# Sample batches of a hybrid decode step: late key tiles on ScalarE's DMA queue, their class ahead of the block sums on TensorE, and two evictions on ScalarE

## The reference

```python
# sparse heads: compressed blocks, selected blocks, window of 512
p_cmp  = softmax(q @ kvc_k.T * SCALE - slope * dist)
imp    = (p_cmp summed over the heads of a group and the blocks' pieces)
top    = top_k(imp + forced, 16)            # 16 of 33 blocks of 64 keys
o_sel  = softmax(q @ k[top].T ...) @ v[top]
o_win  = softmax(q @ k_window.T ...) @ v_window
# dilated heads: (window, dilation) = (128,1), (512,4), (2048,16)
o_dil  = outputs of the three, weighted by their softmax denominators
y      = concat(gates * (o_cmp, o_sel, o_win), o_dil) @ w_out
```

## Time and profile before

| | us |
|---|---|
| median of 3 timed runs | 2613.19 |
| lowest and highest of them | 2601.59, 2617.41 |
| the profiled execution | 2605.86 |
| its span, first to last instruction | 2604.0 |
| busy in it: PE matmul, VectorE, ACT, POOL | 2439.6, 1023.8, 598.9, 504.4 |

### The profile page before, as it was taken

One profiled execution on the slowest core, in us unless ns is written; L12 is line 12 of the kernel. 1 busy time (PEld: TensorE's weight loads), 2 busy tenths in 40 slices (PEclk: granted clock), 3 DMA queues, 4 the chain that ended last, 5 costly groups with the idle time before them and its releaser, 6 DMA issues.

```text
span 2604.0 us, 44719 instructions
## 1 busy us (share of the span) xinstructions
PE 2439.6 (94%) x13806; PEld 1755.9 (67%) x13806; DVE 1023.8 (39%) x3087; ACT 598.9 (23%) x1498; POOL 504.4 (19%) x511
## 2 busy tenths in 40 slices
PE   7998999898989999999999989998898989999998
PEld 4545767676666777777745457677666667777776
DVE  2002776434345322335510147753434442323374
ACT  2101564111112332221111025530111123222202
POOL 0001010000004344434200011000000233433340
PEclk9997999898999999999999989999898999999999
DMA  9622001776775354544365310047676743544541
GB/s 329 232 104 91 1 0 66 259 286 229 289 268 204 133 201 167 198 178 152 150 242 177 134 51 1 0 174 271 227 285 231 283 178 151 199 178 159 202 167 37
DMA packets 126229, 448.23 MB, mean 172 GB/s; under 512 B 17665, under 2 KB 89218, under 8 KB 104962
## 3 DMA queue, kind: packets, MB, share of 16 engines
q1 hardware_dynamic: 118768, 433.23, 45.2%
q10 hardware_dynamic: 7314, 13.20, 1.4%
HBM read 435.76 MB, written 152.57 MB: 226 GB/s over the span
## 4 chain that ended last, share of the span: by engine, by line
PE 77%; SPq 7%; issue 6%; DVE 5%; DMA 3%; ACT 1%; DVEq 0%; ACTq 0%; POOLq 0%
PE bank L963 35%; PE bank L1046 15%; PE bank L1126 5%; SPq L487 4%; SPq L484 4%; PE bank L1154 3%; DMA zone<-in_dilated_k 3%; PE bank L1223 3%; PE bank L1334 2%; PE bank L1139 2%; PE bank L1302 1%; PE bank L1242 1%; PE bank L1369 1%; PE bank L1149 1%; PE bank L944 1%
## 5 line engine op out<-in xcount | busy, mean ns | idle before, releaser
L963 PE MATMUL bank<-zone,ring 128*128 128x288 f32 x1664 | 424.8, 407 | 8.0 <-DVE zone L1512 5.4
L1046 PE MATMUL bank<-ring,hT 128*128 128x512 f32 (+3 forms) x960 | 395.5, 566 | 6.8 <-ACTq L701 5.0
L963 PEld LDWEIGHTS bank<-zone,ring 128*128 128x128 f32 x1664 | 314.8, 190 | 101.0 <-DVE zone L1512 10.9
L963 PE MATMUL bank<-zone,w 128*128 128x288 f32 x1408 | 353.5, 406 | 0.0
L963 PEld LDWEIGHTS bank<-zone,w 128*128 128x128 f32 x1408 | 267.5, 190 | 73.9
L1046 PEld LDWEIGHTS bank<-ring,hT 128*128 128x128 f32 (+1 forms) x960 | 169.4, 181 | 200.6 <-issue 186.4
L1223 PE MATMUL bank<-ring,w 128*128 128x128 f32 x2048 | 239.6, 277 | 0.0
L1223 PEld LDWEIGHTS bank<-ring,w 128*128 128x128 f32 x2048 | 232.1, 192 | 2.4 <-issue 2.4
L812 POOL TENSOR_TENSOR w<-ring 128x512 f32<-128x512 f32 x72 | 97.2, 1350 | 552.0 <-PE bank L963 311.0
L680 ACT ACTIVATE zone<-zone,stat 128x32 f32<-128x32 f32 (+4 forms) x256 | 128.4, 502 | 165.2 <-DVE stat L1658 163.3
L617 ACT COPY zone<-bank 128x288 f32<-128x288 f32 x72 | 28.7, 399 | 562.8 <-PE bank L963 534.7
(11 more groups left out here) (240 smaller groups left out, 2926.9 us busy)
## 6 DMA issues: line engine op xcount, KB each, us to landing
out_dil_s<-in_state_kv_dil SPq DMA_DIRECT2D x48, 2720.0 KB, 11.9
ring<-in_w_units SPq DMA_DIRECT2D x72, 1024.0 KB, 4.8
zone<-in_dilated_v SPq DMA_DIRECT2D x16, 3328.0 KB, 11.2
ring<-in_cache_kv_cmp SPq DMA_DIRECT2D x256, 128.0 KB, 4.4
ring<-in_cache_kv_sel SPq DMA_DIRECT2D x256, 128.0 KB, 5.8
zone<-in_dilated_k SPq DMA_DIRECT2D x32, 1024.0 KB, 7.4
ring<-in_w_in SPq DMA_DIRECT2D x10, 2048.0 KB, 8.0
zone<-in_dilated_k SPq DMA_DIRECT2D x16, 1280.0 KB, 5.5
```

Source lines behind the costliest of these rows:

```text
L963: last = mm(dst[:, 0:HALF], lhs[:, k, :], rhs(k), start=first and k == 0, stop=(k == 3), skip_group_check=True)
L1046: last = mm(dst, hT[:, k, t * P:t * P + ROWS[t]], ring[:, n % 2, k * CH:k * CH + width], start=start and k == 0, stop=stop and k == KT - 1)
```

## The change

Four edits, and the waits that follow from them.

1. The load of the late tiles goes from SP's program to ACT's: at the start of ACT's `batch`, behind a wait for `kda_used`. In SP's program `load_dilated_k_rest` is gone, from the loop and from behind it.
2. On PE the late class stands before the block sums.
3. The copies of PTW and PTD go from VectorE to ACT, behind the exponential of the dilated scores. They raise `ptk_act`; the value products wait for its second count. `bank01_used` now has 3 events for a batch.
4. VectorE waits for the dilated exponential before the two reciprocals, which until now was implied by the copies. PE no longer waits for `bank01_used` before the transposes of the selected probabilities.

```diff
@@ sync
-                def load_dilated_k_rest(b):
-                    sp.wait_ge(kda_used.sem, kda_used.at(l * NB + b, 1))
-                    sp.dma_start(kda[:, 0:4, :], of_batch("dilated_k", b)[:, ND_A + 4:, :]).then_inc(kda_ld.sem, 16)
...
-                    load_raw(page, range(0, 2))
-                    load_dilated_k_rest(b)
-                    load_raw(page, range(2, 9))
+                    load_raw(page, range(0, 9))
...
-                load_dilated_k_rest(NB - 1)
@@ scalar, batch
+                    act.wait_ge(kda_used.sem, kda_used.at(it, 1))
+                    act.dma_start(kda[:, 0:4, :], i["dilated_k"][ds(l, 1), ds(b, 1), :, ND_A + 4:, :].rearrange(
+                        "o q p g f -> (o q p) g f")).then_inc(kda_ld.sem, 16)
                     act.wait_ge(sc_used.sem, sc_used.at(it, SC_S + 1))
                     probs(s_c, 1, low)
...
                     probs(s_d, 3, slice(0, P))
+                    act.wait_ge(td_full.sem, td_full.at(it, TD_PTW + 1))
+                    B = bank[TD_PTW % 2]
+                    copy(ptw[:, 0:4, :].rearrange("p c r -> p (c r)"), B[:, 0:256])
+                    copy(ptw[0:64, 4, :], B[0:64, 256:320]).then_inc(ptk_act.sem, 1)
+                    act.wait_ge(td_full.sem, td_full.at(it, TD_PTD + 1))
+                    B = bank[TD_PTD % 2]
+                    copy(ptd[:, 0:3, :].rearrange("p e r -> p (e r)"), B[:, 0:384])
+                    copy(ptd[0:64, 3, :], B[0:64, 384:512]).then_inc(ptk_act.sem, 1)
@@ tensor, batch
+                    pe.wait_ge(kda_ld.sem, kda_ld.at(it, 2))
+                    dilated_class(ND_A + 4).then_inc(td_full.sem, 1)
                     B = bank[SC_BANK[SC_IMP]]
                     pe.wait_ge(s_gs.sem, s_gs.at(it, 1))
                     pe.sem_inc(waits_taken_pe, 1)
                     mm(B[:, 0:P], gs[:], s_c, start=True, stop=True).then_inc(sc_full.sem, 1)
 
-                    pe.wait_ge(kda_ld.sem, kda_ld.at(it, 2))
-                    dilated_class(ND_A + 4).then_inc(td_full.sem, 1)
...
-                    pe.wait_ge(td_used.sem, td_used.at(it, TD_PTD + 1))
+                    pe.wait_ge(ptk_act.sem, ptk_act.at(it, 2))
...
                     for u in range(2):
-                        pe.wait_ge(td_used.sem, td_used.at(it, TD_PTD + u))
-                        pe.sem_inc(waits_taken_pe, 1)
@@ vector, batch
-                    dve.wait_ge(td_full.sem, td_full.at(it, TD_PTW + 1))
-                    B = bank[TD_PTW % 2]
-                    V.tensor_copy(ptw[:, 0:4, :].rearrange("p c r -> p (c r)"), B[:, 0:256])
-                    V.tensor_copy(ptw[0:64, 4, :], B[0:64, 256:320]).then_inc(td_used.sem, 1)
-                    dve.wait_ge(td_full.sem, td_full.at(it, TD_PTD + 1))
-                    B = bank[TD_PTD % 2]
-                    V.tensor_copy(ptd[:, 0:3, :].rearrange("p e r -> p (e r)"), B[:, 0:384])
-                    V.tensor_copy(ptd[0:64, 3, :], B[0:64, 384:512]).then_inc(td_used.sem, 1)
+                    dve.wait_ge(s_exp.sem, s_exp.at(it, EX_DIL))
+                    dve.sem_inc(waits_taken_dve, 1)
```

More of the change, by code:

```diff
@@ L351, in build @@
         vd_ld = load_sem("dilated_v_loaded", 1)
-        td_full, td_used = ev("bank01_full", TD_N), ev("bank01_used", TD_N - 1)
+        td_full, td_used = ev("bank01_full", TD_N), ev("bank01_used", 3)
         sc_full, sc_used = ev("small_banks_full", SC_N), ev("small_banks_used", SC_N)
@@ L362, in build @@
         oa_full, od_full = ev("sparse_out", 1), ev("dilated_out", 1)
-        pts_act = ev("selected_probs_kept", 1)
+        pts_act, ptk_act = ev("selected_probs_kept", 1), ev("window_dilated_probs_kept", 2)
         out_put = ev("sample_out_kept", 1)
@@ L387, in build @@
                      win_ld, kda_ld, kdb_ld, vd_ld, win_out],
-            "scalar": [c_ld, x_put, sq, h_rdy, w_gain, m1_kept, z_stg, g_exp, hexp_p, a_e, a_pt, s_hexp, s_exp, pts_act, u_relu, u_sq, y_kept[1], *z_out, *fin_out],
+            "scalar": [c_ld, x_put, sq, h_rdy, w_gain, m1_kept, z_stg, g_exp, hexp_p, a_e, a_pt, s_hexp, s_exp, pts_act, ptk_act, u_relu, u_sq, y_kept[1], *z_out, *fin_out],
             "gpsimd": [n_pow, z_v, s_bm, s_comb, a_q, s_q, s_clear, s_pad],
@@ L727, in hidden_exp, with batch @@
                             ACT.Exp, scale=-1.0, bias=ncbias[:, s:s + 1]).then_inc(s_hexp.sem, 1)
-                def batch(it):
+                def batch(b):
+                    it = l * NB + b
                     def probs(scores, n, rows):
@@ L748, in _ @@
                 with act.Fori(0, NB - 1) as b:
-                    batch(l * NB + b)
+                    batch(b)
                     hidden_exp(l * NB + b + 1)
-                batch(l * NB + NB - 1)
+                batch(NB - 1)
                 keep_m1(l, 0)
@@ L1306, in batch @@
                     pe.wait_ge(s_exp.sem, s_exp.at(it, EX_WIN))
-                    pe.wait_ge(td_used.sem, td_used.at(it, max(TD_PTW - 1, 0)))
+                    pe.wait_ge(td_used.sem, td_used.at(it, 1))
                     pe.sem_inc(waits_taken_pe, 1)
@@ L1315, in batch @@
                     pe.wait_ge(s_exp.sem, s_exp.at(it, EX_DIL))
-                    pe.wait_ge(td_used.sem, td_used.at(it, max(TD_PTD - 1, 0)))
+                    pe.wait_ge(td_used.sem, td_used.at(it, 2))
                     B = bank[TD_PTD % 2]
@@ L1364, in batch @@
                         if c == 0:
-                            pe.wait_ge(td_used.sem, td_used.at(it, TD_PTS + 1))
+                            pe.wait_ge(td_used.sem, td_used.at(it, 3))
                         if c == 4:
```

## The result

The kernel with the change takes 2648.12 us (median of 4 runs, 2636.04 to 2653.97), the kernel before on the same chip 2609.67 (4 runs, 2601.59 to 2617.41): the ratio is 1.0137, interval 1.0095 to 1.0179. It is slower by some 38 us (the lower end of the interval is 0.95%), and outside the range of 2584 to 2626. The profiled execution took 2648.57, its span is 2646.7 where it was 2604.0, and the granted clock of TensorE is 0.953 on average where it was 0.964.

What follows compares the result with a forecast made beforehand. SP's queue was taken to set the late tiles' landing, and that the batch. Middle batches -18, first 0, last +15.6 gave -2.4 us against the profiled 2605.86: 2603.5, forecast as 2604, range 2584 to 2626.

Steps and rivals of the forecast that it cites:

- (d): Middle batches: low PE clock on the value products costs 0.8 us, leaving 1.5 gained each, 18 us over 12 batches.
- (e): First batch of each layer: landing maybe 2 us earlier, new PE order costs 2.4 after it; net nothing.
- (f): Last batch of each layer: SP's weight units and state copy delay the tiles 7.0; 7.8 us lost, 15.6 together.
- (a): Ordinary batch: load on ACT's queue issues 2.27 us after early classes, lands 4.8 later; PE's wait becomes 1.0.
- (b): Late class before block sums on PE: shorter wait, but VectorE's block choice, 4.1 us, falls behind the landing.
- (c): Probability copies on ACT, 0.48 and 0.26 us: taken as equal to VectorE's; 2.4 us from choice to value products.
- Rival C: Middle batches gain 0: landing takes 5.5 us and low clock costs 1.7 each time; total 2621 us, chance 0.15.
- Rival B: Last batches: tiles land behind everything, at 786; 11.7 us lost twice, total 2611 us; chance 0.15.
- Rival A: Last batches: tiles hardly held up, landing 776; 1.7 us lost twice, total 2591 us; chance 0.2.

Runs made afterwards that it cites:

- p2: The kernel before with only the copies of the window and dilated probabilities moved to ACT; 2613.9 us, ratio 1.0000.
- e1: The changed kernel, but SP waits for the landing of the last batch's late tiles before issuing weight units and state copy; 2623.8 us, ratio 1.0034.
- e6: The changed kernel with block sums before the late class again and SP waiting for the last batch's tiles before the weight units; 2604.6 us, ratio 0.9968.
- e2: The changed kernel with the 2720 KB state copy moved from weight unit 0 to behind unit 2; 2632.6 us, ratio 1.0083.
- e8: e6 with dilated biasing and compressed-probability copy ahead of VectorE's block choice, PE's half_max product later, second selected scores behind PTW transposes; 2565.0 us, ratio 0.9834.
- e5: e6 with idle matmuls fitted into PE's gaps, two of 512 columns and one of 192 per batch; 2590.9 us, ratio 0.9903.
- p1: The kernel before with only the load of the late tiles moved to ACT's queue; 2622.3 us, ratio 1.0040.
- e4: The changed kernel with the block sums before the late class again on PE; 2621.0 us, ratio 1.0039.
- e10: e6 with one idle matmul of 512 columns per batch ahead of the selected transposes, where PE has no gap; 2605.3 us, ratio 0.9956.

## Why the prediction was wrong

The change of the span was forecast as -2.4 and is +42.7, 45 us more: 13.8 in the middle batches (d), 12.3 in the first ones (e), 12.8 in the last ones (f), and 6.2 outside them, 4.8 of it ahead of the first batch.

(a) was right: the load issued 2.36 after the early classes start (2.27 said), landing 4.85 after it (4.8), wait 1.19 (1.0). (b) and (c) were right in size: from landing to value products 8.6 (9.0 said), ACT's two copies 0.48 and 0.26 to the digit, and p2 shows nothing in all. Two of their terms were off and partly cancel: the late class took 1.08 at the full clock, where 1.9 was read from a batch at the low one, and PTD took up to 0.45 more. The middle batches' value products start 2.5 earlier on average, where 2.3 was said.

(d) is the first step that failed: "Bounds: nothing, or 1.7 us lost with 3.4 us at the low level; I take 0.8". In the middle batches the value products lost 1.8 in their first ten records and PTD 0.2 to 0.45 (up to 1.11 for 0.66). I saw that the low stretch would move onto them and then took half of its price. The stretch is also longer than said, some 7 us in each batch. It fell before on a wait and on short products; now it falls on work of the path, and of the 2.5 won ahead of it some 2.2 are lost again. 12 batches gained 4.2 us together, 18 were forecast. Rival C named this: its low clock on the value products (1.7 each time) and its sign, a pitch still of 44 us, came true, though not its slower landing (5.5).

(e), "nothing", measured 6.1 and 6.2, 12.3 together. "The landing may come 2 us earlier on an emptier queue" was false: the queue is not emptier, SP issues nine raw pages around the load, and the landing took 8.65 us in layer 0, 1.8 longer than before, and 7.89 in layer 1, 0.6 longer. Behind it the choice costs the 2.2 of (b) (value products 20.84 after the early classes for 16.85, 1.8 of it the landing), and then they run at the low clock, 1.8 more, which (e) left out. e1 beside e6 shows 2.5 to 2.8 for the order with its clock. The first batches of e1 and e2, which run the same program there as the changed kernel, take 46.3 to 47.6, so some 2 us of each 6 may be scatter between executions.

(f) said 7.8 in each layer, and it is 14.2 and 14.3. The step that failed is "7.0 more", taken from a store of 128 KB: a load of 1024 KB was held up by 11.4. Rival B, with its landing 15.7 after the issue, was right on this to 0.6 us, though not for its reason, that the tiles land behind everything: unit 1 landed after them; it missed 0.3 of the path behind it and 1.5 of value products at the low clock. Rival A was refuted. The Trainium skill (DMA: Bandwidth & Descriptors, Queues, rings and completion order) has the queues take turns by whole packets. I read that as one turn of delay for the whole load, but each of its packets waits for a turn. With turns of equal size that would be about twice the 4.85 alone, some 10 us (an estimate from that row): the 9.1 of e2 fits, the 16.25 doesn't, and the measurement decides. The same section of the Trainium skill also says that a transfer's semaphore is raised only when every earlier write of that DMA engine is done, whichever queue it came from. By that tiles that come just after a copy from HBM to HBM are told of only when much of the copy has been written. The 9.1 of e2, with the copy gone, fit this, but no run here tells the data's arrival from the semaphore's.

The chances failed in one more way. B and C were priced as alternatives, at 2611 and 2621, although one is of the last batches and the other of the middle ones, and nothing kept both from being true. Together they are 2605.9 + 23.4 = 2629, and with (e) 2642, against 2648.57 for the profiled execution, of which 4.8 lie ahead of the batches. The range's upper end, 2626, was below even the sum of the two.

## What to carry to other kernels

A transfer moved to another queue loses its place in line: write down what the old queue will now issue in its stead, in the first and the last iteration too, and put what isn't urgent behind it. Where the same low stretch of the clock comes back in each iteration, read what it would lie on after the change, and don't count a gain ahead of it until a batch at full clock has been compared with one that isn't. Waits that are split up and shortened (e8) win twice, idle work in a gap (e5) wins some; and rivals that speak of different places in the kernel are to be added, not weighed against each other.

## What the runs showed of the hardware

- The pitch of the batches with a low stretch is nearly the same in kernels whose paths differ: mostly 44.3 to 44.6 before and after, mostly 44.0 to 44.4 in e1, e2, e6 and p1. Where no low stretch lies on the path it follows the work: 41.5 in e4 and e6, 42.5 in e10, 40.8 in e8. In the changed kernel the low stretches are also spaced as the batches are. A batch whose low stretch lies ahead of a wait is as fast as one without (42.45 and 42.46 in e10, 40.90 and 40.79 in e8). What decides whether a batch gets one is open: two batches of e4 with the same waits differ. A rule of the chip for this was not tried further.
- In e5's batch from 585.48 a low stretch of some 3 us begins at 595, with PE at work since 593.07, where it had stood still 1.54 us for gs.
- A load of 1024 KB on ACT's queue took 4.8 to 5.3 us in the middle batches, 6.6 to 8.7 in the first ones with nine raw pages going out on SP's, 9.1 with two weight units there, and 16.3 with those and a copy of 2720 KB from HBM to HBM, all issued in the 2 us ahead of it.
- A matmul of 512 columns, float32 and 128 output rows is 0.91 us at full clock; the value products, with 16 rows each, come to 0.21 us a record.
